# When the first three output products of the second attention block are closed

## The reference, cut to what matters

```python
        qkv = (y @ w_qkv[i]).reshape(B, S, 3, N_HEADS, HEAD_DIM)
        ...
            o = moba_attention(q, k, v, rel_bias)
        h = h + o.transpose(0, 2, 1, 3).reshape(B, S, D) @ w_o[i]
        y = rms_norm_2(h, ffn_norm[i])
        h = h + conv_ffn(y, w_up[i], conv_w[i], conv_b[i], w_down[i])
```

## Time and profile before

| | |
|---|---|
| median of 3 runs | 912.92 us (912.11 to 915.02) |
| the profiled execution's own time | 913.21 us |
| its span in the profile | 911.4 us |
| TensorE matmul busy | 883.0 us, 97% |
| VectorE busy | 668.6 us, 73% |
| ScalarE busy | 504.4 us, 55% |
| GpSimd busy | 65.7 us, 7% |
| mean granted TensorE clock | 0.997 of full speed |

### The profile page before, as it was taken

One profiled execution on the slowest core, in us unless ns is written; L12 is line 12 of the kernel. 1 busy time (PEld: TensorE's weight loads), 2 busy tenths in 40 slices (PEclk: granted clock), 3 DMA queues, 4 the chain that ended last, 5 costly groups with the idle time before them and its releaser, 6 DMA issues.

```text
span 911.4 us, 18632 instructions
## 1 busy us (share of the span) xinstructions
PE 883.0 (97%) x8020; PEld 839.3 (92%) x8020; DVE 668.6 (73%) x1132; ACT 504.4 (55%) x814; POOL 65.7 (7%) x83
## 2 busy tenths in 40 slices
PE   5998999999999999999999999999999999999997
PEld 1797898999898989999999999999888999999997
DVE  3878867566979687677888884678666778888653
ACT  2489667453344637655355444456665567666442
POOL 0100201121001101020000000220000200000011
PEclk9999999999999999999999999999999999999999
DMA  8755332333776664464998889635332536555631
GB/s 334 262 195 185 99 134 97 137 139 97 245 261 229 234 232 165 165 216 183 273 339 300 280 287 262 229 116 192 139 138 92 182 140 214 203 185 177 249 130 47
DMA packets 27681, 177.31 MB, mean 195 GB/s; under 512 B 2864, under 2 KB 5680, under 8 KB 7504
## 3 DMA queue, kind: packets, MB, share of 16 engines
q1 hardware_dynamic: 27600, 176.13, 55.6%
HBM read 174.29 MB, written 1.84 MB: 193 GB/s over the span
## 4 chain that ended last, share of the span: by engine, by line
PE 81%; DVE 8%; ACT 6%; DMA 2%; POOL 1%; issue 1%; SPq 0%; DVEq 0%; ACTq 0%
PE ps L1093 45%; PE ps L1099 22%; PE ps L1091 2%; DVE wl L1841 2%; ACT wh L1454 2%; PE ps L1138 1%; DVE acc L1740 1%; PE ps L1146 1%; PE ps L1232 1%; PE ps L1149 1%; PE ps L1097 1%; PE ps L1252 1%; DMA raw<-in_ada_dram 1%; DMA raw<-in_w_in_dram 1%; DVE KT L1723 1%
## 5 line engine op out<-in xcount | busy, mean ns | idle before, releaser
L1841 DVE TENSOR_TENSOR wl<-raw,wh 128x1024 fp32r<-128x1024 f32 x265 | 321.4, 1232 | 75.1 <-ACT wh L1454 74.4
L1093 PE MATMUL ps<-HH,wh 128*128 128x256 f32 x1480 | 369.5, 286 | 0.7 <-ACT HH L1428 0.2
L1093 PE MATMUL ps<-HH,wl 128*128 128x256 f32 x1480 | 356.4, 277 | 0.0
L1454 ACT ACTIVATE wh<-raw 128x1024 fp32r<-128x1024 f32 x265 | 273.3, 1042 | 140.0 <-PE ps L1099 107.5
L1093 PEld LDWEIGHTS ps<-HH,wh 128*128 128x128 f32 x1480 | 278.8, 188 | 9.4 <-issue 4.3
L1093 PEld LDWEIGHTS ps<-HH,wl 128*128 128x128 f32 x1480 | 278.4, 188 | 1.9 <-issue 1.9
L1099 PE MATMUL ps<-HL,wh 128*128 128x256 f32 x1480 | 225.9, 277 | 0.0
L1099 PEld LDWEIGHTS ps<-HL,wh 128*128 128x128 f32 x1480 | 194.7, 188 | 0.1
L1093 PE MATMUL ps<-FH,wl 128*128 128x256 f32 x352 | 84.5, 276 | 0.0
L1093 PE MATMUL ps<-FH,wh 128*128 128x256 f32 x352 | 84.5, 276 | 0.0
L1740 DVE SCALAR_TENSOR_TENSOR acc<-raw,silc,acc 128x512 f32<-128x512 f32 x101 | 76.3, 756 | 8.1 <-DMA raw<-in_ada_dram 5.0
(11 more groups left out here) (269 smaller groups left out, 1088.9 us busy)
## 6 DMA issues: line engine op xcount, KB each, us to landing
raw<-in_ada_dram SPq DMA_DIRECT2D x32, 1024.0 KB, 5.6
raw<-in_w_fi_dram SPq DMA_DIRECT2D x22, 1024.0 KB, 4.9
raw<-in_w_up_dram SPq DMA_DIRECT2D x22, 1024.0 KB, 4.8
raw<-in_w_rest_dram SPq DMA_DIRECT2D x20, 1024.0 KB, 4.8
raw<-in_w_in_dram SPq DMA_DIRECT2D x16, 1024.0 KB, 4.8
raw<-in_w_qkv_dram SPq DMA_DIRECT2D x12, 1024.0 KB, 4.8
raw<-in_w_o_dram SPq DMA_DIRECT2D x8, 1024.0 KB, 4.9
raw<-in_w_fo_dram SPq DMA_DIRECT2D x8, 1024.0 KB, 5.0
```

What stands on the lines that cost most here:

```text
L1093: e.matmul(o, w[:, k, 128 * t:128 * t + 128], x_hi[:, k0 + k, :], start=first and n + k == 0, **MM)
L1454: e.activation(whl[u % HALF][0][:, 0:n], raw[i % RAW][:, c:c + n], ACT.Copy).then_inc(*a_hi.up(u))
L1841: e.tensor_tensor(wl[:, 0:n], raw[i % RAW][:, c:c + n], wh[:, 0:n].bitcast(F32), ALU.subtract).then_inc(*v_lo.up(u))
```

## The change

The closing calls move into the loop: a product is closed when its second unit has been listed, and no longer after the loop.

```diff
@@ in_turns(ps)
         for n in range(2):
             for p in ps:
                 run_unit(p, n, min(open_units) + HALF - 1)
                 open_units.remove(p["units"][n])
-        for p in ps:
-            close_product(p)
+                if n == 1:
+                    close_product(p)
```

## The result

| | kernel before | changed kernel |
|---|---|---|
| median, first session, 6 executions each | 913.08 us (912.11 to 915.55) | 921.43 us (917.85 to 922.88) |
| ratio | | 1.0069, 95% interval 1.0041 to 1.0096 |
| profiled execution, its span | 911.4 us | 920.1 us |
| mean granted TensorE clock | 0.997 | 0.993 |

The forecast was 911.7 us, with 3% on slower. The changed kernel was 8.35 us slower by the medians, which are in the ratio 1.0091; the ratio in the table is the recorded estimate, with its interval.

What follows compares the result with a forecast made beforehand. TensorE, 97% busy, was taken as the bound; 0.55 us from P0's bank plus 0.65 from the closing chain gave 1.2 us off, hence 912.0 by the profiled execution and 911.7 by the median, range 910.2 to 913.5.

Steps and rivals of the forecast that it cites:

- The bank of P0: Start of P3: P0's residual goes first, so P3 need not wait for its bank; gain 0.66 or 0.46, taken as 0.55 us.
- What waits behind the residuals: VectorE's low parts queued behind the separate residuals: none costs TensorE anything; `wl4` for P2 has 0.65 us of cover.
- The transfer behind `wl4`: Weights for `uv` 0: issued at about 708.5, landing 4.8 us later at 713.3, where `wh4` on ScalarE then begins.
- GpSimd's sums: Sums ahead of the matmul with ones: only P2's two remain after 714.95, ending at about 717.0, in time for P3's end.
- The closing chain: Last residual to logarithm: 1.66 us instead of 2.31 once the sum is in time, a gain of 0.65 us.
- The sum: Total gain of the two terms, 0.55 + 0.65 = 1.2 us, giving 911.7 us for the median.
- what bounds the kernel: TensorE, busy 177.00 of 177 us from 723 to 900, so the stage's gain should reach the end one for one.
- rival 4: TensorE's tile pace, 1.41 then 1.36 us, might change for some 20 tiles: 1 us more gain, 910.7 us; chance 0.07.

Runs made afterwards that it cites:

- only_p0: Kernel before, with only P0 closed in its turn, P1 and P2 after the loop as before; one execution, 914.61 us.
- again2: Changed kernel run a third time, nothing edited, session 3; ratio 0.9976 to the kernel before, 0 of 10 executions above 919 us.
- again5: Changed kernel, nothing edited, second of two runs in session 5; ratio 0.9998, 4 of 12 executions above 919 us.
- warm5: Kernel before, with 5 instead of 9 matmuls on constants ahead of the up projection; 915.58 us, ratio 0.9993.
- gather_before: Kernel before, with the up projection's first matmul waiting for all four HH tiles, so TensorE starts once; 920.75 us, ratio 1.0052.
- nudges: Changed kernel plus one 128-column float32 matmul on constants ahead of every product from `ug` 1 on but `dn` 0; 924.6 us, ratio 1.0122.
- again3: Changed kernel run a fourth time, nothing edited, session 4; ratio 0.9957, 1 of 10 executions above 919 us.
- nudge1: Changed kernel plus one 128-column float32 matmul on constants ahead of `ug` 1 alone; 920.89 us, ratio 1.0025.

## Why the prediction was wrong

Point by point, by its own steps:

- **The bank of P0** (0.55, from 0.46 or 0.66): 0.45. P3 ran at the pace of P2, 1.41 us a tile, which was the lower of the two ends.
- **What waits behind the residuals**: nothing, as forecast. From its residual's start to `wl4`'s it took 0.61, and P2 had no wait.
- **The transfer behind `wl4`**: issued at 711.11, as `wl4` ended; `wh4` waited 1.11 us for it and began 4.7 us later.
- **GpSimd's sums**: forecast 2.05 us from the last squares to their end; it took 2.5 (717.39 to 719.90), with one slow sum of 1.64 us and one of 0.73: a slow and a fast sum together are more than the 2.05 that I took. In time all the same, ahead of the matmul with ones at 720.37.
- **The closing chain** (0.65): 0.63, by the difference to `only_p0`; 722.23 - 720.57 = 1.66 from the last residual, the value of the earlier trace rows.
- **The sum** (1.2): 1.08 in the stage, with P0 to P2 at the slow pitch before and after. At the fast one the stage took 16.95 us in the changed kernel (`again2`, `again5`) and 18.34 in the kernel before (`warm5`, whose edit lies behind it): 1.39. The forecast lies between the two. The pitch of P3 alone doesn't change the stage of the kernel before, which waits for the sum: `gather_before`, with P3 at the slow one, took 18.59 us too.

The step that failed is the last one of the part on what bounds the kernel: from TensorE's 177.00 busy of 177 us I concluded that "what the stage gives or takes should arrive at the end one for one". A busy share of 100% says that TensorE doesn't wait, and not how fast it goes. What the stage hands on is its end, and also the restart of 1580 matmuls, which all run at the pitch that this restart leads to; 117.7 instead of 113.3 ns cost 7.0 us, six times the gain. I had both paces on the table: rival 4 quoted 1.41 and 1.36 us a tile, and in the stage of the change I even saw the pace change at the pause. I priced it for 20 tiles, toward faster only, and did not ask over how many matmuls a pace persists. The range left it out for the same reason. It was narrow in a second way, as its middle rested on three executions: the kernel before had medians of 914.6 to 918.0 us in the later sessions, and of the six later medians of the changed kernel only three (912.6, 912.65, 913.32) lie within 910.2 to 913.5.

What is shown: the 7.04 us of the first comparison's profile are the slow pitch; the pitch is set at a restart and holds to the next interruption; the changed kernel was profiled at either, and the kernel before, profiled at the fast one only, has the same long executions; an edit of one wait moves the share of executions above 919 us from none of 16 to 4 of 6. Inside the stage the change brings what was forecast.

What stays open: why five of six executions of the changed kernel in the first session were above 919 us (the sixth, at 917.85, may have been at either pitch), and none of the six before, where five other sessions had 7 of 66 against 24 of 111. At those shares, five of six is no plausible chance. The shares differed by chip or session, so it may be that the restart that the change moved led to the slow pitch on the first session's chip; that isn't shown, and only one of the six was profiled. Open is also what state in TensorE the two pitches stand for.

## What to carry to other kernels

Look at the distance from start to start of equal matmuls in every long stretch, not at the busy share alone: here two values 4% apart were hidden under 100% busy and a full granted clock. An edit that shifts or reshapes a restart ahead of a long uninterrupted stretch can win or lose more there than in its own stage, so its worth has to be compared at equal pitch, and over several sessions. Six executions of one session that agree with each other may be worth one draw and not six.

## What the runs showed of the hardware that I had not expected

- Two steady distances between 256-column matmuls with their weight loads, 113.3 and 117.8 ns, at a granted clock of 1.00 in both, and none between them in any of the 17 traces. The matmul rows are modelled 276 and 281 ns long.
- One 128-column float32 matmul between two such stretches is enough to change the pitch. In one execution of `nudges`, 23 of them gave slow, slow, fast in turn, without exception.
- A single start after a wait of 1.25 us was profiled at the slow pitch in both kernels, and all 5 executions of one and 4 of 6 of the other were above 919 us. Of the executions of the two kernels with four starts 0.4 us apart, 31 of 177 were, outside the first session.
- The granted clock differs between executions of the same code: from 315 to 345 us it was 0.94 in the changed kernel's first profile and in those of `again3`, `again5`, `nudge1` and `warm5`, and 1.00 in the kernel before and the eleven others. That, with what else varies ahead of 418 us, is the 2.60 us at the beginning:

```profile
315.00:345.00 30.00, 28.67 (x273) 27.28 (x274) 21.70 (x38) 13.05 (x19) 0.00 (x0) 0.94 0.61 211
```

- GpSimd's first sums, forecast at 0.74 us, took 0.89 and 0.93, and each overlapped the low parts a little. The one from 715.77 lay beside the two low parts at 715.61 and took 1.65, and the one from 717.46, which began beside them, took 1.64.
